# Spreading two condition rows over the partitions: by matrix products and copies, or by two broadcast reads

## The reference, cut to what matters

```python
mod = jax.nn.silu(c) @ ada_w[l] + ada_b[l]
sh1, sc1, g1, sh2, sc2, g2 = jnp.split(mod, 6, axis=-1)
h = _modulate(_rmsnorm(x, mix_pre_w[l]), sh1, sc1)     # h * (1 + sc1) + sh1
o = _hybrid_mixer(h, w_in[l], w_out[l], ...)
```

## Time and profile before

| | |
|---|---|
| median of three executions | 3396.64 us |
| the profiled execution, its own time | 3392.56 us |
| its span, first to last instruction | 3390.8 us |
| granted TensorE clock, mean of the span | 0.989 |
| TensorE (PE) busy | 3267.6 us, 96% |
| VectorE (DVE) busy | 2784.9 us, 82% |
| ScalarE (ACT) busy | 1057.2 us, 31% |
| GpSimd (POOL) busy | 1177.3 us, 35% |
| DMA, first of 40 slices (85 us each) | busy 9 tenths or more, 404 GB/s |

### The profile page before, as it was taken

One profiled execution on the slowest core, in us unless ns is written; L12 is line 12 of the kernel. 1 busy time (PEld: TensorE's weight loads), 2 busy tenths in 40 slices (PEclk: granted clock), 3 DMA queues, 4 the chain that ended last, 5 costly groups with the idle time before them and its releaser, 6 DMA issues.

```text
span 3390.8 us, 48513 instructions
## 1 busy us (share of the span) xinstructions
PE 3267.6 (96%) x19317; PEld 2991.7 (88%) x19317; DVE 2784.9 (82%) x3910; ACT 1057.2 (31%) x1414; POOL 1177.3 (35%) x583
## 2 busy tenths in 40 slices
PE   7999999998997999999999999999999999999998
PEld 2688888887995447999999999999999999999997
DVE  6888888888876668978888888888688878888887
ACT  2222232223322002962323323323323323332332
POOL 2443333333440578002323333333133333343331
PEclk9999999999998999999999999999999999999999
DMA  9644444444656311468999999999799989999896
GB/s 404 243 172 155 165 161 158 161 164 149 225 182 255 121 63 63 176 260 312 356 355 357 361 350 345 356 348 370 284 359 352 357 329 352 357 349 355 350 342 243
DMA packets 173329, 916.73 MB, mean 270 GB/s; under 512 B 16175, under 2 KB 53976, under 8 KB 79960
## 3 DMA queue, kind: packets, MB, share of 16 engines
q1 hardware_dynamic: 123894, 555.47, 44.3%
q0 software_dynamic: 49248, 358.63, 27.2%
HBM read 878.41 MB, written 34.55 MB: 269 GB/s over the span
## 4 chain that ended last, share of the span: by engine, by line
PE 76%; DVE 13%; DMA 5%; issue 4%; ACT 1%; POOL 0%; SPq 0%; DVEq 0%; ACTq 0%
PE ps_all L1042 17%; PE ps_all L1103 9%; PE ps_all L1104 9%; PE ps_all L1109 9%; PE ps_all L1049 9%; PE ps_all L1007 6%; PE ps_all L738 4%; PE ps_all L739 4%; PE ps_all L740 4%; DMA sb_col_ring_w<-in_ada_wt 2%; DVE sb_tops L1722 2%; DVE sb_hot L1998 2%; PE ps_all L684 1%; DVE sb_col_ring_w L1726 1%; DVE sb_hot L1995 1%
## 5 line engine op out<-in xcount | busy, mean ns | idle before, releaser
L1405 ACT ACTIVATE sb_raw_hi<-sb_raw_ring 128x2048 fp32r<-128x2048 f32 x256 | 490.9, 1918 | 1158.7 <-DMA sb_raw_ring<-in_v_t 531.9
L1918 DVE TENSOR_TENSOR sb_raw_lo<-sb_raw_ring,sb_raw_hi 128x2048 fp32r<-128x2048 f32 x256 | 585.7, 2288 | 102.0 <-ACT sb_raw_hi L1405 101.8
L1103 PE MATMUL ps_all<-sb_w_hi,sb_raw_hi 128*128 128x342 f32 x2048 | 645.1, 320 | 18.7 <-ACT sb_raw_hi L1405 11.4
L1042 PE MATMUL ps_all<-sb_h_hi,sb_raw_hi 128*128 128x342 f32 x2048 | 646.7, 320 | 10.1 <-issue 6.7
L1042 PE MATMUL ps_all<-sb_h_lo,sb_raw_hi 128*128 128x342 f32 x2048 | 645.8, 320 | 0.0
L1104 PE MATMUL ps_all<-sb_w_lo,sb_raw_hi 128*128 128x342 f32 x2048 | 644.4, 320 | 0.0
L2219 POOL DMA_INDIRECT sb_gather_ring<-in_u_tab,sb_kept x171 | 297.4, 1739 | 757.4 <-DVE sb_kept L2044 579.2
L2219 POOL DMA_INDIRECT sb_gather_ring<-in_v_tab,sb_kept x171 | 312.8, 1829 | 620.1 <-DVE sb_acc_a L2057 407.9
L2148 POOL TENSOR_TENSOR sb_w_low<-sb_w_raw,sb_w_high 128x2048 fp32r<-128x2048 f32 (+1 forms) x64 | 267.3, 4177 | 427.1 <-ACT sb_w_high L1221 427.1
L1103 PEld LDWEIGHTS ps_all<-sb_w_hi,sb_raw_hi 128*128 128x128 f32 x2048 | 388.5, 190 | 20.7 <-ACT sb_raw_hi L1405 12.2
L1042 PEld LDWEIGHTS ps_all<-sb_h_hi,sb_raw_hi 128*128 128x128 f32 x2048 | 385.7, 188 | 11.2 <-issue 10.3
(11 more groups left out here) (295 smaller groups left out, 5485.1 us busy)
## 6 DMA issues: line engine op xcount, KB each, us to landing
sb_raw_ring<-in_u_t SPq DMA_DIRECT2D x128, 1024.0 KB, 7.2
sb_raw_ring<-in_v_t SPq DMA_DIRECT2D x128, 1024.0 KB, 7.6
sb_arena<-in_ada_wt SPq DMA_DIRECT2D x96, 512.0 KB, 4.4
sb_w_raw<-in_w_t SPq DMA_DIRECT2D x32, 1024.0 KB, 4.9
sb_w_raw<-in_w_v SPq DMA_DIRECT2D x32, 768.0 KB, 4.2
sb_g_ring<-table_scratch SPq DMA_DIRECT2D x32, 684.0 KB, 9.8
sb_arena<-in_ada_w SPq DMA_DIRECT2D x10, 2048.0 KB, 12.5
table_scratch<-sb_stage SPq DMA_DIRECT2D x8, 2432.0 KB, 8.1
```

The costliest lines, as they stand in the source:

```text
L1042: last = mm(acc, raw_hi[:, r[0], kk * P:(kk + 1) * P], part[:, kk, :], start=i == 0, stop=False)
L1103: mm(accs[c], v, w_hi[:, slots[e], :], start=e == 0, stop=False)
L1405: acti(raw_hi[:, k % 2, :], raw_ring[:, k % RAW, :], ACT.Copy).then_inc(S["un_hi"], 1)
L1918: vec.tensor_tensor(raw_lo[:, k % RAW, :], raw_ring[:, k % RAW, :], raw_hi[:, k % 2, :].bitcast(f32), ALU.subtract)\
```

## The change

The two broadcast reads and the sync engine's wait ahead of them are gone. TensorE now multiplies `silu_r` (32 x 128) by a column of the identity matrix that is read repeatedly, so that each of the 128 output partitions receives the same row: one product gives 128 numbers of a row on all partitions, 16 products a whole row of 2048 in banks 4 to 7. ScalarE copies the row into `silu_a`. Then the same for the second group, after the first copy. The scratch in HBM is still written, since later stages read it (`silu_b`, `silu_w`).

```diff
             half_load(0)
             half_load(1)
-            sp.wait_ge(S["silu_rows"], 1)
+            sp.wait_ge(S["silu"], 2)
             sp.dma_start(silu_d.rearrange("g (k p) -> (g k) p", p=P), silu_r).then_inc(S["silu_out"], 16)
             for t in range(NT):
                 sp.dma_start(x_sb[:, t, :], x[t * P:(t + 1) * P, :]).then_inc(S["x_in"], 16)
-            sp.wait_ge(S["silu_out"], 16)
-            for g in range(GROUPS):
-                sp.dma_start(silu_a[:, g, :], silu_d[g:g + 1, :].partition_broadcast(P)).then_inc(S["silu_in"], 16)
             dot_load(0)
...
             sp.wait_ge(S["xtr"], KD)
+            sp.wait_ge(S["silu_out"], 16)
             for g in range(GROUPS):
                 sp.dma_start(silu_b[:, g, :], silu_d[g:g + 1, :].partition_broadcast(P)).then_inc(S["silu_in"], 16)
...
-            sp.wait_ge(S["silu_in"], 64)
+            sp.wait_ge(S["silu_in"], 32)
...
-            pe.wait_ge(S["silu"], 1)
+            def silu_rows(g):
+                pe.wait_ge(S["silu"], 2)
+                wait(pe, "silu_act", 2 + g)
+                for kk in range(KD):
+                    pick = ident[0:GROUPS * KD, g * KD + kk:g * KD + kk + 1].to_broadcast([GROUPS * KD, P])
+                    last = mm(psum[:, 4 * NB + kk * P:4 * NB + (kk + 1) * P], pick, silu_r, start=True, stop=True)
+                last.then_inc(S["silu_t"], 1)
+
+            silu_rows(0)
+            silu_rows(1)
             ada_half(0)
...
+            for g in range(GROUPS):
+                act.wait_ge(S["silu_t"], g + 1)
+                acti(silu_a[:, g, :], psum[:, 4 * NB:8 * NB], ACT.Copy).then_inc(S["silu_act"], 1)
...
                 act.wait_ge(S["x_in"], 16 * NT)
+                act.wait_ge(S["silu_act"], 2 + GROUPS)
...
-            dve.wait_ge(S["silu_in"], 32)
+            dve.wait_ge(S["silu_act"], 2 + GROUPS)
```

More of the change, by code:

```diff
@@ L344, in bank @@
             return psum[:, i * NB:(i + 1) * NB]
-        names = """consts rows_in dist_in x_in sumsq silu_e silu colsT cols_ev lg_e
-            silu_rows silu_out silu_in col_in0 col_in1 col_in2 col_in3 col_a col_used late_cols late_t late_row late_out bias_in silu_w gate2_cols gate2_t gate2_bias gate2_row gate2_out
+        names = """consts rows_in dist_in x_in sumsq silu_act silu colsT cols_ev lg_e
+            silu_out silu_in silu_t col_in0 col_in1 col_in2 col_in3 col_a col_used late_cols late_t late_row late_out bias_in silu_w gate2_cols gate2_t gate2_bias gate2_row gate2_out
             half_in0 half_in1 half_in2 half_done ada_ev row_t mod_b mod_p pc_used xtr h_tmp h_high h_low
@@ L1166, in _ @@
             act.wait_ge(S["consts"], 80)
-            acti(silu_e, silu_c, ACT.Exp, scale=-1.0).then_inc(S["silu_e"], 1)
-            acti(silu_re, silu_r, ACT.Exp, scale=-1.0).then_inc(S["silu_e"], 1)
+            acti(silu_e, silu_c, ACT.Exp, scale=-1.0).then_inc(S["silu_act"], 1)
+            acti(silu_re, silu_r, ACT.Exp, scale=-1.0).then_inc(S["silu_act"], 1)
             act.wait_ge(S["colsT"], 1)
@@ L1554, in _ @@
             RSQRT = 11
-            dve.wait_ge(S["silu_e"], 1)
+            dve.wait_ge(S["silu_act"], 1)
             link(vec.tensor_scalar(silu_e, silu_e, 1.0, None, ALU.add))
@@ L1560, in _ @@
             vec.tensor_tensor(silu_c, silu_c, silu_e, ALU.mult).then_inc(S["silu"], 1)
-            dve.wait_ge(S["silu_e"], 2)
+            dve.wait_ge(S["silu_act"], 2)
             link(vec.tensor_scalar(silu_re, silu_re, 1.0, None, ALU.add))
             link(vec.reciprocal(silu_re, silu_re))
-            vec.tensor_tensor(silu_r, silu_r, silu_re, ALU.mult).then_inc(S["silu_rows"], 1)
+            vec.tensor_tensor(silu_r, silu_r, silu_re, ALU.mult).then_inc(S["silu"], 1)
             dve.wait_ge(S["cols_ev"], 1)
```

## The result

The changed kernel takes 3411.25 us (median of 10 runs, 3405.97 to 3417.60) against 3397.39 us for the kernel before (10 runs, 3388.77 to 3404.01). The two medians lie 13.9 us apart. The ratio is 1.0043, with a 95% interval from 1.0033 to 1.0053: +0.43%, or 14.6 us (11.2 to 18.0). The forecast was 3400.6 us with a range from 3391 to 3409, so the time lies 2 us outside it. The profiled execution took 3411.33 us with a span of 3409.5 us, and so stands for the median.

The account below looks back on a forecast made before the run. TensorE's written order was taken to carry the opening, with DMA also full: DMA's -4.9 us worth nothing, +5.1 on TensorE, 0.9 absorbed, +4 us; added to the median 3396.64, 3400.6 us, range 3391 to 3409.

Parts of the forecast that it names:

- TensorE's written order: Opening after the first turn: TensorE's fixed sequence, without DMA waits, passes its delay on; 4 us at the second projection.
- The rival of the relief carried through: Opening's DMA: removing two reads brings pieces sooner and saves 4.9 us at the end, 3391.7 us; chance 0.10.
- the rival of nearly free products: Before half 0: products done when it lands at 11.0 us; price 0 to -2 us, 3394.6 to 3396.6; chance 0.08.
- group 0 5.37: First sixteen added products on TensorE, from 6.7 us: 5.37 us from a cold start, ending at 12.1 us.
- group 1, now with the clock up: 4.1: Second sixteen added products, after ScalarE's copy: 4.1 us at the full clock, from 14.1 to 18.2 us.
- The row that I took as model: Sixteen float32 products of the same output shape in `x_turn` 0 to 3: 5.37 us from a cold start.
- so is the warm start of half 0: Halves 0 and 1 behind the products: counted at the full clock, 13.94 us where they had taken 15.86.
- the bound of 12.0 us: Products at half the clock throughout, 8.2 us a group; the late-buffers rival's shift, 3408.6 us; chance 0.09.
- the 0.9 us absorbed at the end: GpSimd's first weight part: its previous instruction ends 0.9 us after half 9, so 0.9 of the 5.1 us is absorbed.
- landing times close to those of before: Sync engine's queue: loads wait for buffers freed later, so the 4.9 us of DMA relief is spent waiting.
- The overlap of 0 to 2 us: GpSimd's weight part overlaps VectorE's last piece less, which could give back 0 to 2 us.
- the shift of 5.1: End of halves 0 and 1, and everything behind: 32.1 us where before it was 27.0, 5.1 us later.

Follow-up runs that it names:

- second pair: Kernel before and changed kernel, each profiled once more with no edit: 3400.29 us and 3412.93 us.
- full rows: Changed kernel, but its products use all 128 partitions, the unused rows filled with ones that meet zeros: 3405.53 us in one run.
- squares first and one group: Against the kernel before: input squared before evacuation, group 0 as 128-row products directly behind half 1, group 1 read: 3392.74 us, ratio 0.9985.

## Why the prediction was wrong

**Right: what carries the end.** TensorE's written order carried the shift through to the second projection, with no wait for a half behind the first turn. The reads' removal was worth nothing that could be measured in the kernel after (the kernel with reads kept: 3411.86 against 3411.25). The DMA share fell below 1.00, and the queue waited for buffers longer, as said. The rival of the relief carried through fell; the rival of nearly free products fell too (7.2 us a group, where it needed 1.2).

**Wrong: the duration of the two groups**, the term "group 0 5.37" and "group 1, now with the clock up: 4.1". They took 7.21 and 7.16: +1.8 and +3.1 us. The row that I took as model had shape and type in common, but its products fill 128 rows, and those of the change fill 32. Groups with 128 rows took 6.14, 5.43 and, with the clock up, 3.84. The expected 5.37 contained a clock that comes up on the way; for these products it didn't.

**Wrong: "so is the warm start of half 0".** Halves 0 and 1 took 15.40 (and 16.42), not 13.94: +1.5 us, +2.5 in the second profile. For the same reason.

**Wrong: the bound of 12.0 us was thought unlikely.** The shift that I had worked out for half the clock throughout was 12.0; measured were 11.5 at the first turn (47.28 - 35.75) and 11.8 in the second pair. I gave that case 0.09, because a pause of 2 us was near to pauses behind which the clock is up. Both halves of that reason fell: with 32 rows the clock never came up in group 0, so that there was nothing for the pause to keep, and with 128 rows the pause of 2.0 us was followed by clock 0.53. The place within the bounds was chosen from the row that looked alike. That the bound came so near is in part luck. It had 8.2 us a group, where 7.2 were measured (2.0 us too much for both), and a warm start of half 0, which was cold (1.5 us too little). And the range ended at 3409, 0.4 us above that case's own 3408.6, with no room for cold halves or for scatter.

**Missing: what else rides on it.** The first turns stayed cold for 6.79 us instead of 5.37 in this profile, which adds 1.4 at half 2; in the second pair it adds nothing (5.67 and 5.65), so this part is scatter between executions.

**Wrong: the 0.9 us absorbed at the end, and landing times close to those of before.** The change from half 2 to the end is +0.8 us instead (13.75 - 12.95). These are rows of ScalarE, GpSimd and VectorE in the kernel after:

```profile
120.22 1.91 ACT L1233 ACTIVATE sb_w_high<-sb_w_raw 128x2048 fp32r<-128x2048 f32 x1 [4.22 <-DMA sb_w_raw<-in_w_t]
```

```profile
123.78 3.16 POOL L2167 TENSOR_TENSOR sb_h_lo<-sb_ret_out,sb_h_hi 128x512 fp32r<-128x512 f32 x1 [9.78 <-ACT sb_h_hi L1211]
126.90 4.59 POOL L2160 TENSOR_TENSOR sb_w_low<-sb_w_raw,sb_w_high 128x2048 fp32r<-128x2048 f32 x1
```

```profile
126.88 4.64 DVE L1597 TENSOR_SCALAR sb_cols<-sb_tiny,sb_cols 128x2 f32<-128x2 f32 x1
```

The second weight load landed at 120.2 us, 14.8 later than before (105.4). It stands in the sync engine's queue behind halves that wait for TensorE's buffers. So GpSimd's part before the weight part hangs on DMA, but the DMA itself hangs on TensorE: it absorbed nothing and started the weight part at 126.90, 16.0 us later. The overlap of 0 to 2 us was there in this pair, and it gave back 2.05 us (4.59 for 6.64). In the second pair it wasn't: the weight part took 4.60 us before and 4.61 after. The weight part reaches the end through VectorE's last column steps. One of them, 2 numbers a partition, takes 4.64 us and ends with GpSimd's subtraction, where its neighbours take 0.2 to 0.3, and ScalarE goes on only behind it. It takes 4.4 to 4.7 us in each of the 14 profiles.

**The sum with measured sizes.** Groups 7.2 + 7.2 for 5.4 + 4.1 make +4.9; halves +1.5; together the shift of 5.1 becomes 11.5. With 1.4 of cold turns and 0.8 at the end it is 13.75 in the profiles. The timed difference is 14.6 us, with an interval that holds it.

## What to carry to other kernels

Work that is put on TensorE is priced by what the clock does under it and behind it, and not by its count of products alone. Here float32 products that fill 32 of the 128 rows ran at the lower clock at both places that were tried, but for their first 2 us behind the halves, and ahead of the halves they left those to start cold. There they cost 12 to 14 us of the opening. The same products with the unused rows filled and placed in a wait behind full work cost nothing, and it took both. A DMA queue at share 1.00 isn't by itself the limit: while TensorE handed the buffers back later, 2.10 MB less to read was worth nothing that could be measured. Once TensorE is sooner, the next limit may be 0.5 us away. Where a bound from "all at the lower clock" is available and no row shows the very form of the new instruction, it deserves more than the tail of the chances.

## What the runs showed of the hardware that was not expected

- Float32 products of 32 rows, 64 records: 14.37 us from the start of the program (7.21 + 7.16), and 12.42 us right behind halves at clock 1.00, during which the granted clock fell to 0.50 and stayed. With 128 rows, the same 64 records took 7.41 us at clock 1.00. Each of their weight loads and products has the same number of columns.
- Busy share didn't tell the clock: 2.00 of 2.00 us busy in both sets of windows, clock 0.50 in the one and 1.00 in the other. The Trainium skill, "TensorE: Matmul & The Clock Gate", gives for small contractions that one product of 32 rows takes the same time as one of 128 (section "Why this matters for your kernels"). At the same clock the traces agree: both have the pace of 11 or 12 records in 2 us at 0.50. Over a group of products they differ, since the clock that is granted differs: 12.42 us against 7.41.
- The granted clock reads 1.00 until the first change that the trace recorded (26.2 us in the kernel after, 15.1 before, 11.5 with full rows), while instructions run at half the pace (11 records in 2 us, where a row with clock 0.50 has 11 and a row with 1.00 has 18 to 21). From that change on, column and pace agree.
- A pause of 2.67 us behind a group with 128 rows and 0.4 us of small transpositions left the turns at full pace (3.84 us, squares first and one group), one of 3.85 us didn't (6.68 us). In between nothing was tried. A pause of 2.0 us behind a group that had only just sped up was followed by clock 0.53 (full rows, group 1).
- GpSimd's 2048-wide subtraction takes 4.59 us alone and 6.64 us where it starts beside VectorE's last piece; the same piece of VectorE takes 3.23 us beside GpSimd and 2.29 alone. An instruction of VectorE on 2 numbers a partition takes 4.64 us beside that subtraction and ends with it (131.52 against 131.49 us), and 0.2 to 0.3 us otherwise.
